# Attention head by head in straight order, with the two maximum products of a unit in one two-bank buffer

## What is computed

```python
def one_block(qblk):
    s = jnp.einsum('bqhd,bkhd->bhqk', qblk, k, preferred_element_type=jnp.float32) * scale
    p = jax.nn.softmax(s, axis=-1)
    return jnp.einsum('bhqk,bkhd->bqhd', p.astype(v.dtype), v)
```

## Time and profile before

| | us |
|---|---|
| median of 3 runs | 3671.3 |
| lowest and highest | 3663.44, 3674.0 |
| the profiled execution | 3671.86 |
| its span | 3670.1 |
| first maximum of attention to its last GpSimd fold | 509.1 to 1803.81 |

### The profile page before, as it was taken

How to read it: one execution, slowest core, us unless ns; L and a number is a source line. 1 busy time by engine, 2 the same in 40 slices (tenths; PEclk the granted TensorE clock), 3 DMA queues, 4 the chain that set the end, 5 groups by cost and what they waited for, 6 DMA issues and landing times. The chain is left out here.

```text
span 3670.1 us, 48958 instructions
## 1 busy us (share of the span) xinstructions
PE 3348.8 (91%) x16108; PEld 2745.4 (75%) x16108; DVE 2017.9 (55%) x3007; ACT 1582.6 (43%) x2396; POOL 1389.7 (38%) x914
## 2 busy tenths in 40 slices
PE   8969969999999999998779898997999969799899
PEld 7968847776776767776578687885888858688787
DVE  4457768888887878886557333113332337622211
ACT  4446637776776767776545222002222225412100
POOL 1147838887887878887511000000000011000000
PEclk9979979999999999998889899998999979899999
DMA  7769961222122212224243897655222245398555
GB/s 279 257 232 311 315 179 40 53 51 53 32 52 52 53 47 53 53 53 97 84 169 121 253 293 241 205 186 185 87 94 94 91 157 185 121 266 238 177 187 172
DMA packets 457298, 538.22 MB, mean 147 GB/s; under 512 B 55705, under 2 KB 372505, under 8 KB 437393
## 3 DMA queue, kind: packets, MB, share of 16 engines
q1 hardware_dynamic: 457104, 535.81, 47.6%
HBM read 324.98 MB, written 210.61 MB: 146 GB/s over the span
## 5 line engine op out<-in xcount | busy, mean ns | idle before, releaser
L1267 POOL TENSOR_TENSOR at_acc<-at_acc,at_ph 128x1024 f32<-128x1024 f32 x288 | 690.4, 2397 | 84.6 <-ACT at_ph L1193 70.2
L1301 DVE TENSOR_TENSOR at_pl<-at_sc,at_ph 128x1024 fp32r<-128x1024 f32 x408 | 498.0, 1221 | 184.4 <-ACT at_sc L1194 162.1
L1193 ACT ACTIVATE at_ph<-at_sc 128x1024 fp32r<-128x1024 f32 x408 | 418.8, 1027 | 398.1 <-PE at_sc L1113 397.7
L1287 DVE TENSOR_REDUCE at_mx<-at_mxp 128x1 f32<-128x512 f32 x816 | 521.8, 680 | 31.7 <-PE at_mxp L1124 29.0
L1194 ACT ACTIVATE at_sc<-at_sc 128x1024 f32<-128x1024 f32 x408 | 416.3, 1020 | 0.0
L1109 PE MATMUL at_sc<-at_qt,at_kt 97*128 97x512 f32 x816 | 337.7, 414 | 53.4 <-DMA at_qt<-at_neg 26.0
L1111 PE MATMUL at_sc<-at_qt,at_kt 96*128 96x512 f32 x816 | 330.1, 405 | 0.0
L1113 PE MATMUL at_sc<-at_qt,at_kt 96*128 96x512 f32 x816 | 329.1, 403 | 0.0
L1138 PE MATMUL at_o_hi<-at_ph,at_v 128*128 128x512 f32 x816 | 325.0, 398 | 1.5 <-DVE at_half L1306 1.5
L1140 PE MATMUL at_o_lo<-at_pl,at_v 128*97 128x512 f32 x816 | 323.4, 396 | 0.0
L1124 PE MATMUL at_mxp<-at_kt,at_qt 96*128 96x512 f32 x816 | 279.5, 415 | 29.6 <-DMA at_kt<-kT 23.0
(11 more groups left out here) (246 smaller groups left out, 7412.3 us busy)
## 6 DMA issues: line engine op xcount, KB each, us to landing
ma_h<-hT SPq DMA_DIRECT2D x40, 1024.0 KB, 4.8
ogT<-ga_st SPq DMA_DIRECT2D x160, 256.0 KB, 3.5
ou_o<-ogT SPq DMA_DIRECT2D x40, 1024.0 KB, 6.1
ga_h<-hT SPq DMA_DIRECT2D x64, 512.0 KB, 7.3
hT<-lat_n_h SPq DMA_DIRECT2D x24, 1024.0 KB, 6.3
hT<-sg_n_h SPq DMA_DIRECT2D x24, 1024.0 KB, 3.8
qT<-hd_stq SPq DMA_DIRECT2D x60, 384.0 KB, 6.0
kT<-hd_stk SPq DMA_DIRECT2D x120, 192.0 KB, 3.5
```

The lines of the kernel that those rows point to most:

```text
L1193: act.activation(ph[:, g], sc[g % 2][:], ACT.Exp, scale=SCALE).then_inc(p_hi, 1)
L1267: pool.tensor_tensor(acc[:, c.slot, :], f32(ph[:, (g - 1) % 4]).rearrange("p b n -> p (b n)") if t == 1 else acc[:, c.slot, :], now, ALU.a ...
L1287: dve.tensor_reduce(mx[:, n:n + 1], mxp[n % 2][:], AX.X, ALU.max).then_inc(mx_in, 1)
L1301: dve.tensor_tensor(pl[:, g], sc[g % 2][:], f32(ph[:, g]), ALU.subtract).then_inc(p_lo, 1)
```

## The change

1. The order of the chunks: for each head its four prompt chunks and then its sample chunk. `kt` and `v` hold all 2560 keys of a head, and one load each brings them; k's high and low half are two DMAs with a semaphore each, and the maxima wait only for the high half.
2. No hardware loop: all 60 chunks are written out.
3. The maxima run 22 products (11 units) ahead of the scores everywhere, over the borders of chunks.
4. The two single-bank buffers `mxp[0]`, `mxp[1]` are one two-bank buffer. TensorE waits for the reduction of the previous pair before the first of its two products and signals after the second; VectorE reduces both banks in one instruction, 128x2x512 to 128x2. For the first pairs, before any scores, the two score buffers take turns as maximum buffers.
5. On SyncE the row is issued ahead of the store around a sample chunk (`early`), both for the sample chunk and for the prompt chunk behind it.

```diff
 class Chunk:
-    PROMPTS, LAST = NH * PROMPT // BLK, NH * (PROMPT + SAMPLE) // BLK - 1
+    PARTS = TOK // BLK
+    COUNT = NH * PARTS
+    UNITS, ADDS, PIECES = 34, 29, 68
+    LEAD = 22
...
 def run_chunks(eng, step):
-    for k in range(8):
-        step(Chunk(0, k))
-    with eng.Fori(1, Chunk.PROMPTS // 8 - 1) as j:
-        for k in range(8):
-            step(Chunk(j, k))
-    for n in range(Chunk.PROMPTS - 8, Chunk.LAST + 1):
-        step(Chunk(0, n))
+    for n in range(Chunk.COUNT):
+        step(Chunk(n))
 
 def max_pieces(c, t):
-    if c.pairs == 2:
-        ahead, pieces = c.ahead(2), (2 * t, 2 * t + 1)
-    elif t < 5:
-        ahead, pieces = c.ahead(1), (2 * t + 6, 2 * t + 7)
-    else:
-        ahead, pieces = c.ahead(2), (2 * t - 10, 2 * t - 9)
-    return ahead, [n for n in pieces if ahead.exists() and n < ahead.pieces]
+    at = 2 * (c.g0 + t) + Chunk.LEAD
+    head, rest = at // Chunk.PIECES, at % Chunk.PIECES
+    ahead = Chunk(head * Chunk.PARTS + min(rest // 16, Chunk.PARTS - 1))
+    return ahead, [at - ahead.mx0, at - ahead.mx0 + 1] if ahead.exists() else []
...
-        kt = s.sb("kt", [QK + 1, 2, 2, PROMPT], F32R)
+        kt = s.sb("kt", [QK + 1, 2, 2, TOK], F32R)
-        v = s.sb("v", [P, 2, 16, VR + 1], F32R)
+        v = s.sb("v", [P, 2, TILES, VR + 1], F32R)
...
-        mxp = [s.ps(f"mxp{u}", [P, BLK]) for u in range(2)]
+        mxp = s.ps("mxp", [P, 2, BLK])
...
+        def max_buffer(pair):
+            return sc[pair % 2] if pair < 8 or pair == 9 else mxp
+
+        def max_free(pair):
+            return pair - 1 if pair < 8 else {8: 0, 9: 8, 10: 9}.get(pair, pair)
...
+                def load_k(head):
+                    for a, sem in ((0, kh_load), (1, kl_load)):
+                        sp.dma_start(f32(kt[0:QK, head % 2, a]), kT[a, head * QK:(head + 1) * QK, :]
+                                     ).then_inc(sem[head % 2], 16)
...
-                    if c.sample and nxt.exists():
+                    early = c.sample or nxt.sample
+                    if early and nxt.exists():
                         row(nxt)
                     if has_before(c):
-                        store(prev)
-                    if not c.sample and nxt.exists():
+                        store(before(c, 1))
+                    if not early and nxt.exists():
                         row(nxt)
...
                 def maximum(c, pieces):
                     for n in pieces:
                         if n == 0:
-                            pe.wait_ge(q_load[c.quad], c.load * 16 + 16)
-                            pe.wait_ge(k_load[c.kv], loaded(c, 2))
-                        after(pe, mx_in, c.mx0 + (n - 1))
+                            pe.wait_ge(q_load[c.quad], c.turn * 16 + 16)
+                            pe.wait_ge(kh_load[c.kv], loaded(c))
+                        pair = (c.mx0 + n) // 2
+                        if n % 2 == 0:
+                            after(pe, mx_in, max_free(pair))
...
-                                  stop=True).then_inc(mx_mm, 1)
+                        if n % 2 == 1:
+                            m.then_inc(mx_mm, 1)
...
                 def maxima(c, pieces):
-                    for n in pieces:
-                        dve.wait_ge(mx_mm, c.mx0 + (n + 1))
-                        dve.tensor_reduce(mx[:, n:n + 1], mxp[n % 2][:], AX.X, ALU.max).then_inc(mx_in, 1)
+                    for n in pieces[::2]:
+                        dve.wait_ge(mx_mm, (c.mx0 + n) // 2 + 1)
+                        dve.tensor_reduce(mx[:, n:n + 2], max_buffer((c.mx0 + n) // 2)[:], AX.X, ALU.max).then_inc(mx_in, 1)
```

More of the change, by code:

```diff
@@ L873, with __init__ @@
 class Chunk:
-    PROMPTS, LAST = NH * PROMPT // BLK, NH * (PROMPT + SAMPLE) // BLK - 1
[L879 to L885, removed]
+    PARTS = TOK // BLK
+    COUNT = NH * PARTS
+    UNITS, ADDS, PIECES = 34, 29, 68
+    LEAD = 22
+    def __init__(self, n):
+        self.n, self.head, self.part = n, n // self.PARTS, n % self.PARTS
+        self.sample = self.part == self.PARTS - 1
@@ L898, in __init__ @@
-        self.g0_mod = (2 * m) % 4 if self.sample else 0
-        self.half = j * 4 + k // 2
-        self.tile0 = 4 * self.part if self.sample else 0
+        self.slot, self.quad, self.kv = n % 2, n % 4, self.head % 2
+        self.half, self.turn = n // 2, n // 4
+        self.g0 = self.head * self.UNITS + 8 * self.part
+        self.sum0 = self.head * self.ADDS + 7 * self.part
+        self.mx0 = self.head * self.PIECES + 16 * self.part
+        self.tile0 = PT_TILES if self.sample else 0
+        self.after_sample = n > 0 and self.part == 0
@@ L925, in max_pieces, with unit @@
-def max_pieces(c, t):
-    if c.pairs == 2:
-        ahead, pieces = c.ahead(2), (2 * t, 2 * t + 1)
-    elif t < 5:
-        ahead, pieces = c.ahead(1), (2 * t + 6, 2 * t + 7)
-    else:
-        ahead, pieces = c.ahead(2), (2 * t - 10, 2 * t - 9)
-    return ahead, [n for n in pieces if ahead.exists() and n < ahead.pieces]
+    return Chunk(c.n - by)
+def unit(g):
+    head, rest = g // Chunk.UNITS, g % Chunk.UNITS
+    c = Chunk(head * Chunk.PARTS + min(rest // 8, Chunk.PARTS - 1))
+    return c, g - c.g0
@@ L973, in attention, with loaded @@
         o_out = [s.sem(f"o_out{u}") for u in range(2)]
[L974 to L980, removed]
+        def loaded(c):
+            return (c.head // 2 + 1) * 16
         def stored(c):
@@ L1021, in load_v @@
[L1021 to L1031 removed]
+                    sp.dma_start(f32(qt[0:QK, c.quad]),
+                                 qT[c.head, :, :, c.part * BLK:(c.part + 1) * BLK].rearrange("a d t -> d a t")
+                                 ).then_inc(q_load[c.quad], 16)
@@ L1040, in sum_rows @@
                 def sum_rows(c, which):
-                    if c.sample:
-                        h = c.n - c.PROMPTS
-                        return sums_out[which, h:h + 1, PROMPT:TOK]
-                    return sums_out[which, bass.ds(c.load, 1), c.part * BLK:(c.part + 1) * BLK]
+                    return sums_out[which, c.head:c.head + 1, c.part * BLK:(c.part + 1) * BLK]
                 def store(c):
@@ L1104, in scores @@
                         pe.wait_ge(row_in[c.slot], c.half * 64 + 64)
-                    g = (c.g0_mod + t) % 2
+                        if c.part == 0:
+                            pe.wait_ge(kl_load[c.kv], loaded(c))
+                    g = (c.g0 + t) % 2
+                    if c.n == 0 and t < 2:
+                        pe.wait_ge(mx_in, 7 if t == 0 else 10)
                     after(pe, p_lo, c.g0 + (t - 1))
@@ L1150, in total @@
                     m.then_inc(tot_mm, 1)
-                pe.wait_ge(const_in, 4)
-                c0 = Chunk(0, 0)
+                pe.wait_ge(const_in, 5)
+                c0 = Chunk(0)
                 maximum(c0, range(c0.pieces))
-                maximum(c0.ahead(1), range(6))
+                maximum(c0.ahead(1), range(Chunk.LEAD - 16))
                 scores(c0, 0)
```

129 lines of the change are left out of this document (45 added, 84 removed).

## The result

The changed kernel takes 3615.42 us (median of 4 runs, 3613.50 to 3615.68) against 3672.59 us before: a ratio of 0.9848, 95% interval 0.9831 to 0.9865. That is 57.2 us less where 61.5 were forecast, inside the range. The profiled execution has a span of 3613.2 us against 3670.1.

A forecast was written before the change was run, and what follows sets the result against it. Attention was taken as bound by TensorE's issue in the prompts, by something else in the sample tail, where scores wait for a DMA. -34.4 - 40.3 + 12.2 + 3 - 2 = -61.5, from 3671.9 to 3610.4 us; range 3595 to 3652.

The forecast's parts named there:

- The loop goes, -34.4: Attention's 47 chunks up to the last prompt chunk: writing them out straight saves 34.4 us, mostly three loop turns.
- The sample chunk among the prompts, -40.3: Twelve sample chunks, moved behind their head's prompts, cost 6.12 us each instead of 9.48, a gain of 40.3 us.
- the walk: Step-by-step timing of TensorE through a head's end, from the last prompt chunk's unit 7 into the next head.
- S(s0): The six score products of the sample chunk's unit 0 on TensorE, put at 3.88 to 5.28 us.
- S(q0): The six score products of unit 0 in the next head's first chunk, put at 10.44 to 11.84 us.
- The row's margin: At the next head's first scores: the row lands at 8.7 to 10.2 us, wanted at 10.44; close, but it holds.
- late rows: Rival, 14%: rows behind bulk loads land late, each sample chunk still costs 9.48 us, the 40.3 don't come: 3651.
- The shared buffer, +12.2: One two-bank maximum buffer makes TensorE wait at unit 7: 0.26 us in each of 47 prompt chunks, +12.2 us.
- The +0.12 from unit 4: Unit 4's reduction waits for the second product; the delay runs through neg and two subtractions to unit 7, +0.12 us.
- Start, +3, and end, -2: Attention's start: row behind larger loads, scores about 530, +3 (-6 to +6); its end: last 11 units without maxima, -2.

The follow-up runs named there:

- the straight code alone: Kernel before with only the loop removed, all 60 chunks written out in the old order with two single buffers: 3634.3 us, 0.9898.
- the run with late rows: Changed kernel with the row never issued ahead of the store around a sample chunk: 3738.4 us, 1.0193 against the kernel before.
- the one with the scores ahead: Changed kernel with the next chunk's first score products moved ahead of unit 7's two maximum products on TensorE: 3582.8 us, 0.9759.

## Why the prediction was right, step by step

*The loop goes, -34.4*: shown, 34.6 by the straight code alone. The first chunk was called cold; its distance of 24.67 us was granted 1.00, so that isn't the reason, but it stays, as was said (24.83 in the changed kernel).

*The sample chunk among the prompts, -40.3*: the walk gave 6.56 us from S(s0) to S(q0); the trace has 632.98 - 626.42 = 6.56. By the folds, the kernel with the banks one by one, which has all of the change but the shared buffer, needs 1174.19 us from first to last; the sum without the buffer's term gives 1251.11 - 34.4 - 40.3 - 2 = 1174.4. That it fits so well is in part luck, since the old tail, 113.78 us in this trace, is 118.05 and 117.5 in the two others that have it. And the terms fit less well than their sum: with the banks one by one a sample chunk costs 7.89 + 21.57 - 23.45 = 6.01 us and not 6.12, so the twelve gain 41.6 us and not 40.3. The row's margin held, and the run with late rows shows that it was the condition for all of it. The price set for late rows, 40 us, was far too low: the rival took the tail's wait, but ahead of the store of a full prompt chunk GpSimd's join comes later, and it costs 123.

*The shared buffer, +12.2*: right in sign and kind, short in size, 15.97 us by the folds and 14.8 by the medians. The step that failed is the one that let the reduction wait for both products only at unit 4. At unit 6, where it counts, the pair and the subtraction ahead of the reduction are, in the kernel before:

```profile
596.01 0.61 PE L1124 MATMUL at_mxp<-at_kt,at_qt 96*128 96x512 f32 x2
...
595.38 1.22 DVE L1301 TENSOR_TENSOR at_pl<-at_sc,at_ph 128x1024 fp32r<-128x1024 f32 x1
```

There the reduction had started at 596.53, about 0.12 us after the first product's end and before the second's; in the trace it now starts at 624.51, with the second product, 1.28 us after the subtraction instead of 1.15. The +0.12 from unit 4 doesn't reach unit 7. In the third chunk, where the join stands behind unit 4, its reduction does start 0.23 us later than with single banks, but the subtraction behind it starts 597.08 - 578.76 = 18.32 us after the chunk's first score product, and with single banks 601.89 - 583.58 = 18.31: the delay is gone by then. And a pair that has waited takes 626.42 - 625.88 = 0.54 us instead of 0.47. So it is 0.17 + 0.13 + 0.07 = 0.37 there, and by the folds 0.33 to 0.36 in the prompt chunks, also in the last of a head, which had been given 0.17.

*Start, +3, and end, -2*: the first fold came 3.5 us later, the first score product at 530.49 where 530 was said. The row behind the loads is shown by moving them. That the size fits is luck as much as skill, since the same start had its first fold at 554.44 in the run with late rows and at 561.94 in the one with the scores ahead. The -2 at the end did not come: the last prompt chunk takes 22.16 us, with the banks one by one 22.14, but it took 22.21 in the old order too. The sample chunks, cheaper than forecast, make up for most of it.

*The time*: 3610 forecast, 3615.4 measured. Of the 4.1 us between 61.5 and 57.4 the buffer has 3.8 and the start 0.5; the other terms together were 0.2 better than forecast, their errors cancelling.

## What to carry to other kernels

Look for the one place in a repeated list where two uses of a buffer stand closest together, and count what lies between them; that, not the mean load of the engine that frees it, says what a merged buffer costs, and here it could be moved apart for nothing (28.7 us by the folds and 32.7 by the medians, for exchanging two steps of one list). A small DMA on which the bound engine waits goes ahead of everything on its queue that waits for others, and ahead of bulk loads that nobody needs yet. An average of 55% busy for VectorE said nothing about either; the fold distances, a clock inside the kernel, told the terms that repeat in each chunk to a tenth of a microsecond. The terms that come once, the start and the old tail, scatter by several us between executions and can't be read from one trace.

## What the runs showed of the hardware that had not been expected

A reduction of two banks at once takes 1218 ns and two of one bank 1.28 us end to end: joining them saves 0.06 us and not a fixed cost of 0.14, since the second one starts 0.6 us after the first. Two maximum products behind a wait take 0.54 us instead of 0.47. The turn of the loop costs 7 to 10 us, is not the same in two kernels with the same products in the loop, and stops different engines in them. A wait of TensorE of 8.4 us was followed by at least 5 us at 1.2 GHz; at the start, behind waits of 11.82 and 2.60 us, the clock was at 0.50 before the scores began. And SyncE was held for 11.8 us at issuing four DMAs of half a kilobyte with the bulk loads of two heads ahead of them, and for 2.5 us with those of one.
